# Output stages of a two-layer decoder trunk: three last slabs interleaved by token tile, and four next slabs split during the norm

## The chip, the cores and the metric

The kernel runs on one core of one Trainium2 chip. The metric is the device time of one execution in microseconds (us). The names used are TensorE (PE, with its weight loads PEld), VectorE (DVE), ScalarE (ACT), GpSimd (POOL) and SyncE (SP), which issues the loads of the weight stream.

## The reference

For each of two layers, on x of 512 tokens by 1024 features in float32:

```python
proj = x @ w_in[l]                      # then three mixers: state-space, pooling, sparse attention
merged = sum(gate * branch_d)           # per-channel sigmoid gates
x = layer_norm(ALPHA * x + merged @ w_out[l], g, b)
h_gate, h_up = split(x @ ffn_w_in[l])   # 2816 wide each
x = layer_norm(ALPHA * x + (silu(h_gate) * h_up) @ ffn_w_out[l], g, b)
```

There are four products that end in a layer norm (n = 0 to 3): the two output stages of each layer.

## The kernel before

Every engine has its own program, with an order written out by hand; each runs its instructions strictly in that order, and semaphores tie them together. Nothing is planned at run time.

**The weight stream.** All large weights come as 264 slabs of 128 x 1024 float32 (512 KB), numbered through both layers. SP loads slab c + 2 into `raw[c % 2]` as soon as VectorE has made the low part of slab c (line 396). Products are made of float32r parts: ScalarE copies a slab into `whi` (`split_hi`, line 973), VectorE subtracts (`split_lo`, line 1373) and writes `wlo`. Both have two slots, by the parity of the slab. `split_hi(c)` waits until TensorE is done with slab c - 2 (`slab_done`). A product of a slab takes 24 matmuls: high by high, high by low, low by high.

**The output stage** (`to_tokens`, line 587). The result is wanted by token: four token tiles of 128 tokens, and two feature halves of 512 columns, so eight PSUM banks. Slabs hold weights of two blocks of input rows for one feature half. All slabs of half 0 come first, then those of half 1. A slab visits the four token tiles with 6 matmuls each (`token_products`). Only the last two slabs (called a and b in the code) are interleaved: a and b on tiles 0 and 1, a on tiles 2 and 3, b on tile 2, the turn-back of tokens 0 and 1, b on tile 3.

**The norm** (`ln_part`, lines 1009 and 1478) runs beside that. Half 0 means token tiles 0 and 1, half 1 tiles 2 and 3. VectorE takes the statistics of a tile's second 512 columns (`second_stats`), aggregates, ScalarE takes the root (`deviations`), VectorE inverts (`scalars`); then VectorE normalizes the first 512 columns (`first_columns`) and ScalarE the others (`normalized`; in half 1 of a norm that is not the last, both). `turn_back` (line 575) transposes 16 blocks to feature order in PSUM, ScalarE applies gain and shift (`gained`, line 997), VectorE splits x into `xh` and `xl` (`halves`, line 1461). Each gives four quarters of two feature blocks.

**The next slabs.** The first two slabs after a norm are computed by quarters (`first_pair`, `x_quarter`, line 543): 6 matmuls of 256 columns each, as soon as a quarter of x for one half of the tokens is split. Order: four quarters of slab 0, turn-back of half 1, four of slab 1, then the second half's four of slab 0 and four of slab 1. The splits of these two slabs stand inside `ln_part`; those of the following two stand after it. Then come whole slabs (`x_slab`, line 537).

**POOL in layer 1.** Behind the norm n = 1, POOL issues the loads of `w1` (2 x 2 MB, read by the compression products, line 673) when the last slab of layer 0 is done, then the store of x to memory when the norm is done, then computes the powers of the state-space poles (lines 476 to 506, `lam` and `eph`). VectorE reads them for matrices and for the scan (line 1687), whose result TensorE multiplies at lines 736 and 742.

Of the kernel before, what the change touches and what calls it, by code (L numbers as in the profile page):

```python
# [16 lines left out]
D, S, L, P = 1024, 512, 2, 128  # L17
# [55 lines left out]
def build_program(nc, wstream, w1s, smalls, norms, consts, xin, pos, out):  # L73
# [45 lines left out]
    gates = place("gates", big_at, [P, 16, S])  # L119
    xt = place("xt", xf_at, [P, 4, D])  # L120
# [134 lines left out]
    with ctx:  # L255
# [155 lines left out]
        def _(pool):  # L411
# [44 lines left out]
            for l in range(L):  # L456
# [69 lines left out]
        def _(pe):  # L526
# [16 lines left out]
            def x_quarter(n, half, g, x_before):  # L543
# [4 lines left out]
                for k in (2 * g, 2 * g + 1):  # L548
                    wh, wl = whi[:, n % 2, k * P:k * P + P], wlo[:, n % 2, k * P:k * P + P]
# [14 lines left out]
            def token_products(slot, fh, t, k0, hi, lo, last):  # L564

                dst = ps[:, tile_bank(fh, t), :]
                for q in range(2):
                    a, b = hi[:, k0 + q, P * t:P * t + P], lo[:, k0 + q, P * t:P * t + P]
                    wh, wl = whi[:, slot, S * q:S * q + S], wlo[:, slot, S * q:S * q + S]
# [17 lines left out]
            def to_tokens(n, at, pairs, hi, lo, freed, taken, each, rt):  # L587

                for fh in range(2):
# [3 lines left out]
                    for s in range(pairs - 2 * fh):  # L593
# [4 lines left out]
                        for t in range(4):  # L598
                            m = token_products(c % 2, fh, t, 2 * s, hi, lo, fh == 0 and s == pairs - 1)
# [1548 lines left out]
```

## Time and profile before

| | |
|---|---|
| timed runs | 1765.88 us median of 3 (1765.68 to 1766.67) |
| span of the profiled execution | 1767.2 us (the profile gives no other time of this execution) |
| TensorE matmul busy | 1733.0 us (98%), 10172 instructions |
| VectorE busy | 944.0 us (53%) |
| ScalarE busy | 649.2 us (37%) |
| POOL busy | 125.6 us (7%) |
| mean granted TensorE clock | 0.997 |

Times are from the start of the span. Matmuls are pipelined: one lasts 0.39 us in the trace, while the next starts earlier, so spacing between starts is what counts. The granted clock is a share of 2.4 GHz.

### The profile page before, as it was taken

What the parts mean: (1) busy time and instruction counts of PE and PEld (TensorE: products, weight loads), DVE (VectorE), ACT (ScalarE), POOL (GpSimd) and SP (SyncE); (2) the same over time, 40 slices, a digit from 0 to 9 for tenths busy, and PEclk for the clock granted to TensorE, in tenths of its full rate; (3) what the DMA queues carried; (4) which work ended last, traced back from release to release, by engine and by line L of the source; (5) the groups of instructions that cost most, each with busy time, mean ns of one, the idle gap of its engine ahead of it and who ended that gap; (6) DMA issues with size and microseconds to landing.
All of it is one profiled execution on the core that took longest, in us unless ns stands there. A gap on an engine that the chain in (4) does not pass through costs nothing.

```text
span 1767.2 us, 26801 instructions
## 1 busy us (share of the span) xinstructions
PE 1733.0 (98%) x10172; PEld 1409.5 (80%) x10172; DVE 944.0 (53%) x1514; ACT 649.2 (37%) x1152; POOL 125.6 (7%) x252
## 2 busy tenths in 40 slices
PE   7999999999999999999999999999999999999998
PEld 6778777788888888888888777777888888888886
DVE  5788778444354444422358877775453544444223
ACT  4333666422252222221353346664222522222112
POOL 4700000000000000000037000000000000000000
PEclk9999999999999999999999999999999999999999
DMA  7443111133513222222263431112233222222222
GB/s 259 157 117 88 53 50 49 49 101 102 169 63 105 95 95 95 95 96 95 91 244 110 116 86 50 53 37 72 96 119 119 82 98 95 95 95 95 96 96 83
DMA packets 65918, 174.88 MB, mean 99 GB/s; under 512 B 14256, under 2 KB 26576, under 8 KB 65056
## 3 DMA queue, kind: packets, MB, share of 16 engines
q1 hardware_dynamic: 40192, 140.53, 24.5%
q10 hardware_dynamic: 21888, 13.64, 3.2%
q0 software_dynamic: 3744, 19.41, 3.2%
q8 instruction: 66, 1.08, 0.3%
q14 instruction: 28, 0.23, 0.1%
HBM read 162.27 MB, written 7.08 MB: 96 GB/s over the span
## 4 chain that ended last, share of the span: by engine, by line
PE 86%; DVE 7%; DVEq 3%; ACT 2%; issue 1%; DMA 0%; ACTq 0%
PE ps L532 19%; PE ps L534 18%; PE ps L533 18%; PE ps L572 6%; PE ps L570 6%; PE ps L571 6%; PE ps L857 2%; PE ps L844 2%; PE ps L830 1%; DVE wlo L1376 1%; PE ps L550 1%; PE ps L561 1%; PE ps L552 1%; PE ps L551 1%; PE ps L583 1%
## 5 line engine op out<-in xcount | busy, mean ns | idle before, releaser
L532 PE MATMUL ps<-xh,whi 128*128 128x512 f32 x1312 | 520.0, 396 | 8.4 <-ACT gates L1190 5.1
L534 PE MATMUL ps<-xh,wlo 128*128 128x512 f32 x1312 | 511.3, 390 | 0.0
L533 PE MATMUL ps<-xl,whi 128*128 128x512 f32 x1312 | 510.9, 389 | 0.0
L1376 DVE TENSOR_TENSOR wlo<-raw,whi 128x1024 fp32r<-128x1024 f32 x264 | 324.9, 1231 | 347.4 <-ACT whi L977 338.2
L977 ACT ACTIVATE whi<-raw 128x1024 fp32r<-128x1024 f32 x264 | 278.9, 1057 | 351.0 <-PE ps L572 234.3
L532 PEld LDWEIGHTS ps<-xh,whi 128*128 128x128 f32 x1312 | 246.4, 188 | 61.4 <-issue 7.8
L534 PEld LDWEIGHTS ps<-xh,wlo 128*128 128x128 f32 x1312 | 246.3, 188 | 52.3
L533 PEld LDWEIGHTS ps<-xl,whi 128*128 128x128 f32 x1312 | 246.6, 188 | 48.8 <-issue 0.5
L570 PE MATMUL ps<-whi,hh 128*128 128x512 f32 x352 | 137.5, 391 | 0.0
L572 PE MATMUL ps<-whi,hl 128*128 128x512 f32 x352 | 137.0, 389 | 0.0
L571 PE MATMUL ps<-wlo,hh 128*128 128x512 f32 x352 | 137.0, 389 | 0.0
L1360 ACT ACTIVATE hh<-fb 128x512 f32 (+1 forms) x44 | 27.8, 632 | 201.8 <-DVE fb L1382 201.8
L1382 DVE TENSOR_TENSOR fb<-fa,ps 128x512 f32<-128x512 f32 x44 | 30.2, 687 | 110.9 <-PE ps L534 110.7
L416 POOL TENSOR_TENSOR carry<-carry 1x1 f32<-1x1 f32 x21 | 5.2, 248 | 1176.2 <-PE ps L572 419.5
L1977 DVE SCALAR_TENSOR_TENSOR fa<-ft,ps 128x512 f32<-128x512 f32 x44 | 30.3, 688 | 99.5 <-ACT ft L1357 99.5
L572 PEld LDWEIGHTS ps<-whi,hl 128*128 128x128 f32 x352 | 66.1, 188 | 13.8
L570 PEld LDWEIGHTS ps<-whi,hh 128*128 128x128 f32 x352 | 66.1, 188 | 13.7 <-DVE wlo L1376 0.3
L571 PEld LDWEIGHTS ps<-wlo,hh 128*128 128x128 f32 x352 | 66.1, 188 | 13.6
L1357 ACT ACTIVATE ft<-ps 128x512 f32<-128x512 f32 x44 | 26.3, 598 | 132.7 <-PE ps L534 128.7
L1255 ACT ACTIVATE prob<-ps,tiny 128x128 f32<-128x128 f32 (+3 forms) x128 | 66.3, 525 | 20.4 <-DVE tiny L1802 20.3
L1802 DVE TENSOR_REDUCE tiny<-ps 128x2 f32<-128x256 f32 (+3 forms) x64 | 52.4, 819 | 11.8 <-PE ps L833 11.8
L550 PE MATMUL ps<-xh,whi 128*128 128x256 f32 x128 | 39.5, 309 | 15.7 <-DVE wlo L1376 9.9
(338 smaller groups left out, 2335.5 us busy)
## 6 DMA issues: line engine op xcount, KB each, us to landing
raw<-wstream SPq DMA_DIRECT2D x264, 512.0 KB, 3.3
w<-w1s POOLq DMA_DIRECT2D x4, 2048.0 KB, 11.7
sm<-smalls POOLq DMA_DIRECT2D x2, 1060.0 KB, 6.7
xt<-xin ACTq DMA_DIRECT2D x4, 512.0 KB, 6.3
scratch_u<-pa ACTq DMA_DIRECT2D x8, 256.0 KB
toep<-scratch_k ACTq DMA_DIRECT2D x4, 512.0 KB
toep_b<-scratch_k ACTq DMA_DIRECT2D x4, 512.0 KB
xt<-xin POOLq DMA_DIRECT2D x4, 512.0 KB, 4.0
```

What stands on the lines that cost most here:

```text
L532: pe.matmul(ps[:, bank, :], wh, hi[:, k, :], start=first and i == 0, stop=False)
L533: pe.matmul(ps[:, bank, :], wh, lo[:, k, :], start=False, stop=False)
L534: m = pe.matmul(ps[:, bank, :], wl, hi[:, k, :], start=False, stop=last and i == len(blocks) - 1)
L550: pe.matmul(dst, wh, xh[:, k, cols], start=k == 0, stop=False)
L570: pe.matmul(dst, a, wh, start=False, stop=False)
L571: pe.matmul(dst, a, wl, start=False, stop=False)
L572: m = pe.matmul(dst, b, wh, start=False, stop=last and q == 1)
L844: m = pe.transpose(ps[:, bank, at + P * k:at + P * k + P], prob[:, i % 3, kv, P * k:P * k + P], ident)
L977: act.activation(whi[:, c % 2, :], raw[:, c % 2, :], ACT.Copy).then_inc(hi_ready, 1)
L1255: x = act.activation(prob[:, i % 3, kv, 0:n], ps[:, sbank(i) + kv, 0:n], ACT.Exp, bias=tiny[:, 28 + 8 * (i % 3) + kv:29 + 8 * (i % 3) + kv ...
L1376: dve.tensor_tensor(wlo[:, c % 2, :], raw[:, c % 2, :], whi[:, c % 2, :].bitcast(f32), SUB).then_inc(lo_ready, 1)
L1802: dve.tensor_reduce(tiny[:, 28 + 8 * (i % 3):30 + 8 * (i % 3)], ps[:, sbank(i):sbank(i) + 2, 0:n], AX.X, MAX, negate=True).then_inc(s_max, 1)
```

## The change

The two parts of slab storage get three further slots, `whi_end` and `wlo_end`, in memory that the stage has finished with. The last slab of a stage goes to slot 0, the first two slabs after it to slots 1 and 2; all three are split before the norm's instructions on ScalarE and VectorE. The two slabs after those (b+3, b+4) are split inside the norm, in the ordinary slots. On TensorE the last three slabs are interleaved: tiles 0 and 1 of each, then tile 2 of all, the turn-back of half 0, then tile 3 of all. The pair after it takes the first quarter of its second slab ahead of the turn-back of half 1, and visits both slabs quarter by quarter in the second half. In half 1, VectorE normalizes the first columns, as in half 0. POOL stores x first and loads `w1` after slab 1 of layer 1. The last stage has no next slabs. Layer 0's first pair keeps its order (`first_slabs`). The diff, without the edits that only pass arguments or repeat one shown:

```diff
@@ -117,6 +117,8 @@
+    whi_end = place("whi_end", big_at, [P, 3, 1024], f32r)
+    wlo_end = place("wlo_end", big_at + 3072, [P, 3, 1024], f32r)
@@ -465,13 +467,11 @@
                 if l:
-                    wait(slab_done, l * NSLAB + 2)
-                    load_w1()
-
-                if l:
                     wait(ln_x, l * 16)
                     for t in range(4):
                         pool.dma_start(scr_x[:, t, :], xt[:, t, :]).then_inc(x_stored, 16)
+                    wait(slab_done, l * NSLAB + 4)
+                    load_w1()
@@ -546,7 +546,10 @@
-                    wh, wl = whi[:, n % 2, k * P:k * P + P], wlo[:, n % 2, k * P:k * P + P]
+                    if x_before:
+                        wh, wl = whi_end[:, 1 + n % 2, k * P:k * P + P], wlo_end[:, 1 + n % 2, k * P:k * P + P]
+                    else:
+                        wh, wl = whi[:, n % 2, k * P:k * P + P], wlo[:, n % 2, k * P:k * P + P]
@@ -574,8 +577,7 @@
-                if half == 0 or n == 2 * L - 1:
-                    pe.wait_ge(ln_first, n + half + 1)
+                pe.wait_ge(ln_first, n * 2 + half + 1)
                 pe.wait_ge(ln_second, n * 4 + 2 + 2 * half)
@@ -590,43 +592,57 @@
-                    for s in range(pairs - 2 * fh):
+                    for s in range(pairs - 3 * fh):
                         c = at + fh * pairs + s
                         pe.wait_ge(lo_ready, c + 3)
...
-                a, b = at + 2 * pairs - 2, at + 2 * pairs - 1
-                k = 2 * pairs - 4
-                pe.wait_ge(lo_ready, a + 3)
-                for t in (0, 1):
-                    token_products(a % 2, 1, t, k, hi, lo, False)
-                pe.wait_ge(lo_ready, b + 3)
-                for t in (0, 1):
-                    token_products(b % 2, 1, t, k + 2, hi, lo, True).then_inc(t_psum, 1)
-                for t in (2, 3):
-                    m = token_products(a % 2, 1, t, k, hi, lo, False)
-                m.then_inc(slab_done, 1)
-                token_products(b % 2, 1, 2, k + 2, hi, lo, True).then_inc(t_psum, 1)
+                b = at + 2 * pairs - 1
+                ends = ((whi[:, (b - 2) % 2, :], wlo[:, (b - 2) % 2, :]), (whi[:, (b - 1) % 2, :], wlo[:, (b - 1) % 2, :]), (whi_end[:, 0, :], wlo_end[:, 0, :]))
+                k = 2 * pairs - 6
+                for s in range(3):
+                    pe.wait_ge(lo_ready, b - 2 + s + 3)
+                    for t in (0, 1):
+                        m = token_products(ends[s][0], ends[s][1], 1, t, k + 2 * s, hi, lo, s == 2)
+                        if s == 2:
+                            m.then_inc(t_psum, 1)
+                for s in range(3):
+                    m = token_products(ends[s][0], ends[s][1], 1, 2, k + 2 * s, hi, lo, s == 2)
+                m.then_inc(t_psum, 1)
                 turn_back(n, 0, rt)
-                token_products(b % 2, 1, 3, k + 2, hi, lo, True).then_inc(slab_done, 1)
+                for s in range(3):
+                    token_products(ends[s][0], ends[s][1], 1, 3, k + 2 * s, hi, lo, s == 2).then_inc(slab_done, 1)
+
...
             def first_pair(n, at, rt):
 
-                pe.wait_ge(lo_ready, at + 3)
+                pe.wait_ge(lo_ready, at + 4)
                 for g in range(4):
                     x_quarter(at, 0, g, n * 8)
-                if n:
-                    turn_back(n - 1, 1, rt)
-                pe.wait_ge(lo_ready, at + 4)
+                x_quarter(at + 1, 0, 0, n * 8)
+                turn_back(n - 1, 1, rt)
+                for g in range(1, 4):
+                    x_quarter(at + 1, 0, g, n * 8)
                 for g in range(4):
-                    x_quarter(at + 1, 0, g, n * 8)
-                for c in range(2):
-                    for g in range(4):
+                    for c in range(2):
                         m = x_quarter(at + c, 1, g, n * 8)
-                    m.then_inc(slab_done, 1)
+                        if g == 3:
+                            m.then_inc(slab_done, 1)
@@ -634,7 +650,10 @@
-                first_pair(l * 2, l * NSLAB, xt)
+                if l:
+                    first_pair(l * 2, l * NSLAB, xt)
+                else:
+                    first_slabs()
@@ -976,6 +995,26 @@
+            def split_end_hi(c, slot, free):
+
+                act.wait_ge(raw_loaded[c % 2], (c // 2 + 1) * 16)
+                act.wait_ge(slab_done, free + 3)
+                act.activation(whi_end[:, slot, :], raw[:, c % 2, :], ACT.Copy).then_inc(hi_ready, 1)
...
+            def split_next_hi(c, free):
+
+                act.wait_ge(raw_loaded[c % 2], (c // 2 + 1) * 16)
+                act.wait_ge(slab_done, free + 3)
+                act.activation(whi[:, c % 2, :], raw[:, c % 2, :], ACT.Copy).then_inc(hi_ready, 1)
...
+            def stage_splits(at, pairs, last):
+
+                b = at + 2 * pairs - 1
+                split_end_hi(b, 0, b - 3)
+                if not last:
+                    split_end_hi(b + 1, 1, b - 3)
+                    split_end_hi(b + 2, 2, b - 3)
@@ -989,10 +1028,8 @@
-                    for fh in (0, 1) if half and n < 2 * L - 1 else (1,):
-                        x = act.activation(rt[:, t, S * fh:S * fh + S], ps[:, tile_bank(fh, t), :], ACT.Identity,
-                                           bias=lnnb[:, t:t + 1], scale=lnrs[:, t:t + 1])
-                    x.then_inc(ln_second, 1)
+                    act.activation(rt[:, t, S:], ps[:, tile_bank(1, t), :], ACT.Identity, bias=lnnb[:, t:t + 1], scale=lnrs[:, t:t + 1])\
+                       .then_inc(ln_second, 1)
@@ -1011,16 +1048,16 @@
                 deviations(n, 0)
                 normalized(n, 0, rt)
-                if not last:
-                    split_hi(0, next_slab)
                 for g in range(4):
                     gained(n, 0, g, rt, last)
+                if not last:
+                    split_next_hi(next_slab + 2, next_slab - 2)
                 deviations(n, 1)
-                if not last:
-                    split_hi(0, next_slab + 1)
                 normalized(n, 1, rt)
                 for g in range(4):
                     gained(n, 1, g, rt, last)
+                if not last:
+                    split_next_hi(next_slab + 3, next_slab - 2)
@@ -1063,9 +1100,11 @@
-                a1_split(1)
+                if l == 0:
+                    a1_split(1)
                 a1_out(1)
-                a1_split(2)
+                if l == 0:
+                    a1_split(2)
@@ -1342,15 +1381,16 @@
-                for c in range(1, NO):
+                for c in range(1, NO - 1):
                     split_hi(0, l * NSLAB + OO + c)
                     if c == 1:
                         merged_hi(3)
+                stage_splits(l * NSLAB + OO, KD // 2, False)
                 ln_part(l * 2, l * NSLAB + OF, xt)
...
-                        if not (first and c == 0):
+                        if not first or c == 3:
@@ -1363,8 +1403,9 @@
-                for c in range(1, NG):
+                for c in range(1, NG - 1):
                     split_hi(0, l * NSLAB + OG + c)
+                stage_splits(l * NSLAB + OG, KF // 2, l == L - 1)
@@ -1374,6 +1415,11 @@
+            def split_end_lo(c, slot):
+
+                dve.wait_ge(hi_ready, c + 1)
+                dve.tensor_tensor(wlo_end[:, slot, :], raw[:, c % 2, :], whi_end[:, slot, :].bitcast(f32), SUB).then_inc(lo_ready, 1)
@@ -1490,25 +1536,18 @@
                 first_columns(0)
                 second_stats(n, 2, next_slab + 2)
-                if not last:
-                    split_lo(0, next_slab)
-                halves(n, 0, 0, rt, last)
-                if last:
-                    halves(n, 0, 1, rt, last)
+                for g in range(4):
+                    halves(n, 0, g, rt, last)
                 second_stats(n, 3, next_slab + 2)
                 variances(1)
-                if last:
-                    scalars(n, 1)
-                    first_columns(1)
-                    halves(n, 0, 3, rt, last)
-                else:
-                    halves(n, 0, 1, rt, last)
-                    scalars(n, 1)
-                    for g in (2, 3):
-                        halves(n, 0, g, rt, last)
-                    split_lo(0, next_slab + 1)
+                scalars(n, 1)
+                first_columns(1)
+                if not last:
+                    split_lo(0, next_slab + 2)
                 for g in range(4):
                     halves(n, 1, g, rt, last)
+                if not last:
+                    split_lo(0, next_slab + 3)
@@ -1562,11 +1601,10 @@
-                a1_lo(1)
                 if l == 0:
+                    a1_lo(1)
                     angles()
-                a1_lo(2)
-                if l == 0:
+                    a1_lo(2)
@@ -1956,20 +1994,25 @@
-                def stage(at, pairs, last_low=False):
-                    for c in range(1, 2 * pairs):
+                def stage(at, pairs, last_low=False, last=False):
+                    b = at + 2 * pairs - 1
+                    for c in range(1, 2 * pairs - 1):
                         if c == pairs + 1:
                             first_stats(at + pairs + 2)
                         split_lo(0, at + c)
                         if c == 1 and last_low:
                             low_parts(3)
+                    split_end_lo(b, 0)
+                    if not last:
+                        split_end_lo(b + 1, 1)
+                        split_end_lo(b + 2, 2)
```

## Rows read from the trace of the kernel before

**Rows 1.** The list of waits of TensorE: engine, line, releaser: us in total, times, longest.

```profile
PE ps L550 <- DVE xl L1382: 5.6, 8, 1.3
```

**Rows 2.** ScalarE in order of time (start us, us, what, wait and releaser), splits of b-1, b.

```profile
493.14 1.06 ACT L977 ACTIVATE whi<-raw 128x1024 fp32r<-128x1024 f32 x1 [6.14 <-PE ps L572]
...
864.20 1.06 ACT L977 ACTIVATE whi<-raw 128x1024 fp32r<-128x1024 f32 x1 [4.38 <-PE ps L572]
...
1368.24 1.06 ACT L977 ACTIVATE whi<-raw 128x1024 fp32r<-128x1024 f32 x1 [6.14 <-PE ps L572]
1373.68 1.06 ACT L977 ACTIVATE whi<-raw 128x1024 fp32r<-128x1024 f32 x1 [4.38 <-PE ps L572]
```

**Rows 3.** TensorE in order of time, the first full slab after each of three norms.

```profile
528.41 0.50 PE L532 MATMUL ps<-xh,whi 128*128 128x512 f32 x1
...
899.75 0.50 PE L532 MATMUL ps<-xh,whi 128*128 128x512 f32 x1
...
1402.59 0.50 PE L532 MATMUL ps<-xh,whi 128*128 128x512 f32 x1
```

**Rows 4.** TensorE in order of time, the turn-back of half 1 in the first norm.

```profile
517.86 1.91 PE L583 MATMUL ps<-cn,xt 128*128 128x128 f32 x16
519.52 0.36 PE L550 MATMUL ps<-xh,whi 128*128 128x256 f32 x1
```

**Rows 5.** Windows: stretch, its us, busy us of each engine (instructions), granted clock, DMA share, GB/s.

```profile
514.20:517.60 3.40, 3.40 (x16) 3.10 (x15) 3.14 (x5) 2.76 (x4) 0.00 (x0) 0.50 0.02 5
1760.10:1763.50 3.40, 3.40 (x16) 3.04 (x15) 1.59 (x4) 1.79 (x4) 0.00 (x0) 0.50 0.39 130
1763.50:1764.00 0.50, 0.04 (x1) 0.00 (x0) 0.42 (x1) 0.25 (x1) 0.00 (x0) 1.00 0.87 277
```

**Rows 6.** VectorE in order of time, the first norm.

```profile
494.23 1.23 DVE L1376 TENSOR_TENSOR wlo<-raw,whi 128x1024 fp32r<-128x1024 f32 x1 [4.74 <-ACT whi L977]
...
504.01 0.70 DVE L1443 BATCH_NORM_STATS2 lnst<-ps 128x6 f32<-128x512 f32 x1 [0.39 <-PE ps L572]
...
505.83 1.53 DVE L1483 TENSOR_SCALAR xt<-ps,lnmv,lnrs 128x512 f32<-128x512 f32 x2
```

**Rows 7.** ScalarE in order of time, the gains of half 1 in the first norm.

```profile
518.49 3.75 ACT L1006 ACTIVATE xt<-ps,nrm 128x256 f32<-128x256 f32 x8 [1.53 <-PE ps L583]
```

**Rows 8.** SP's loads of slabs (line 396) from 480 to 532 us.

```profile
DMA to landing us min/median/max: 3.1/3.2/3.3
```

**Rows 9.** POOL in order of time, layer 1, and the powers' last instruction in layer 0.

```profile
882.33 0.18 POOL L416 TENSOR_TENSOR carry<-carry 1x1 f32<-1x1 f32 x1 [419.54 <-PE ps L572]
...
898.49 1.25 POOL L416 TENSOR_TENSOR carry<-carry 1x1 f32<-1x1 f32 x1 [14.94 <-issue]
...
910.75 0.18 POOL L416 TENSOR_TENSOR carry<-carry 1x1 f32<-1x1 f32 x1 [8.90 <-issue]
...
964.96 0.13 POOL L506 MEMSET r8m<- 128x16 f32 x1
...
92.14 0.13 POOL L506 MEMSET r8m<- 128x16 f32 x1
```

**Rows 10.** VectorE in order of time, matrices and scan of layer 1.

```profile
943.93 1.11 DVE L1382 TENSOR_TENSOR tb<-lam,bch 128x512 f32<-128x512 f32 x1
...
965.81 0.68 DVE L1382 TENSOR_TENSOR tb<-lam,bch 128x512 f32<-128x512 f32 x1
...
977.28 1.42 DVE L1382 TENSOR_TENSOR sct<-eph,ps 128x256 f32<-128x256 f32 x4 [0.16 <-issue]
```

**Rows 11.** TensorE in order of time: compression (L673) and Toeplitz (L736) products, both layers.

```profile
65.99 1.36 PE L673 MATMUL ps<-w,zb 128*64 128x256 f32 x10
...
109.01 1.15 PE L736 MATMUL ps<-toep,u 128*64 128x64 f32 x32 [0.66 <-issue]
...
941.92 1.36 PE L673 MATMUL ps<-w,zb 128*64 128x256 f32 x10
...
983.33 1.15 PE L736 MATMUL ps<-toep,u 128*64 128x64 f32 x32 [0.27 <-issue]
```

More of the change, by code:

```diff
@@ L562, in residual, with token_products @@
                                   start=m == 0, stop=False, is_transpose=True)
-            def token_products(slot, fh, t, k0, hi, lo, last):
+            def token_products(high, low, fh, t, k0, hi, lo, last):
                 dst = ps[:, tile_bank(fh, t), :]
@@ L568, in token_products @@
                     a, b = hi[:, k0 + q, P * t:P * t + P], lo[:, k0 + q, P * t:P * t + P]
-                    wh, wl = whi[:, slot, S * q:S * q + S], wlo[:, slot, S * q:S * q + S]
+                    wh, wl = high[:, S * q:S * q + S], low[:, S * q:S * q + S]
                     pe.matmul(dst, a, wh, start=False, stop=False)
@@ L598, in to_tokens @@
                         for t in range(4):
-                            m = token_products(c % 2, fh, t, 2 * s, hi, lo, fh == 0 and s == pairs - 1)
+                            m = token_products(whi[:, c % 2, :], wlo[:, c % 2, :], fh, t, 2 * s, hi, lo, fh == 0 and s == pairs - 1)
                         m.then_inc(slab_done, 1)
-                a, b = at + 2 * pairs - 2, at + 2 * pairs - 1
-                k = 2 * pairs - 4
-                pe.wait_ge(lo_ready, a + 3)
-                for t in (0, 1):
-                    token_products(a % 2, 1, t, k, hi, lo, False)
@@ new lines, in to_tokens, with first_slabs @@
+                for s in range(3):
+                    m = token_products(ends[s][0], ends[s][1], 1, 2, k + 2 * s, hi, lo, s == 2)
+                m.then_inc(t_psum, 1)
+                turn_back(n, 0, rt)
+                for s in range(3):
+                    token_products(ends[s][0], ends[s][1], 1, 3, k + 2 * s, hi, lo, s == 2).then_inc(slab_done, 1)
+            def first_slabs():
+                pe.wait_ge(lo_ready, 3)
+                for g in range(4):
+                    x_quarter(0, 0, g, 0)
+                pe.wait_ge(lo_ready, 4)
+                for g in range(4):
+                    x_quarter(1, 0, g, 0)
+                for c in range(2):
+                    for g in range(4):
+                        m = x_quarter(c, 1, g, 0)
+                    m.then_inc(slab_done, 1)
@@ L624, in first_pair @@
                 for g in range(4):
-                    x_quarter(at + 1, 0, g, n * 8)
-                for c in range(2):
-                    for g in range(4):
+                    for c in range(2):
                         m = x_quarter(at + c, 1, g, n * 8)
-                    m.then_inc(slab_done, 1)
+                        if g == 3:
+                            m.then_inc(slab_done, 1)
             ident = cnv("ident")
@@ L1492, in ln_part @@
                 second_stats(n, 2, next_slab + 2)
[L1493 to L1497 removed]
+                for g in range(4):
+                    halves(n, 0, g, rt, last)
                 second_stats(n, 3, next_slab + 2)
                 variances(1)
[L1500 to L1509 removed]
+                scalars(n, 1)
+                first_columns(1)
+                if not last:
+                    split_lo(0, next_slab + 2)
                 for g in range(4):
                     halves(n, 1, g, rt, last)
+                if not last:
+                    split_lo(0, next_slab + 3)
             dve.memset(tiny[:, 0:1], 0.0).then_inc(lo_ready, 2)
@@ L1971, in ff_pairs @@
                     for c in range(4):
-                        if not (first and c == 0):
+                        if not first or c == 3:
                             split_lo(h, c + 1)
@@ L1991, in _ @@
                     ff_pairs(hl_ + OF // 2 + 2 + i * 2, i + 1, False)
-                stage(l * NSLAB + OG, KF // 2)
+                stage(l * NSLAB + OG, KF // 2, last=l == L - 1)
                 ln_part(l * 2 + 1, (l + 1) * NSLAB, xt)
```

## Prediction

> **What bounds the kernel now.** I read the page first: TensorE is busy 98% of the span, so only what stands between its matmuls, or what slows them, can be taken away. Next the list of waits: in the norms TensorE waits for the split x, 5.6 us in 8 waits [rows 1]. Then the order of time at each norm. Call b the last slab of an output stage, b-1 and b-2 the two before, b+1 to b+4 the next four. ScalarE's split of b-1 is released when slab b-3 is done; I call that moment T: 493.14, 864.20 and 1368.24 for the first three norms [rows 2]. The first full slab after the norm starts at 528.41, 899.75 and 1402.59 [rows 3]. So the stretch takes 35.27, 35.55 and 34.35 us.
>
> Its pure work: three slabs of 24 matmuls at 5.44 us each (1368.24 to 1373.68, one slab [rows 2]) = 16.32; 16 quarters of 6 matmuls, 256 columns each, at 8.89/72 = 0.1235 (519.52 to 528.41 [rows 3, 4], hand-over included) = 11.85; two blocks of 16 transposes, 1.66 each (517.86 to 519.52 [rows 4]) = 3.32. Sum 31.5 us. What is above it is 3.8, 4.05 and 2.85 us of idle time and slow clock. In the first norm the granted clock is 0.50 from 514.20 to 517.60, that is 1.2 of 2.4 GHz, right after its waits for x [rows 5].
>
> **The change, part by part.**
>
> *The weave (TensorE).* No matmul is added or removed; 72 + 96 + 32 instructions stay in each stretch. New order from T: token tiles 0 and 1 of all three slabs (36 matmuls, 8.16 us), tile 2 of all (18, 4.08), the turn-back of half 0, tile 3 of all (18, 4.08), then five quarters, turn-back of half 1, three quarters, eight quarters. Before, only 6 matmuls (1.36 us) stood between turn-back and the first quarter, which needs the turned, gained and split x; now 18 do. Work in three slots means that b-1 must be split by T+2.72. Its low part began at 494.23 and takes 1.23 [rows 6]: T+2.3. It fits, with 0.4 us to spare.
>
> *Splits of b, b+1, b+2 ahead of the norm (ScalarE, VectorE, SP).* Both engines are in order, and the three splits now stand before the first statistics. The high part of b follows that of b-1 at once, its low part runs T+2.2 to T+3.45. Each low part releases SP's load of the slab two later; issue to landing is 3.2 us [rows 8]. b+1: issue T+2.5, landing T+5.7, high part to T+6.8, low part to T+8.1. b+2: issue T+3.65; the two transfers overlap, I take landing T+7.1, high part to T+8.2, low part to T+9.45. Only then does VectorE take the first statistics. Their data are there at T+6.8, so they are 2.7 us late. From the start of the second statistics (504.01) to the end of the first columns (505.83 + 1.53) it takes 3.35 us [rows 6]; the first statistics add 0.97 (0.70, the aggregate and its gaps). The turn-back can start at T+9.45+0.97+3.35 = T+13.8. TensorE is there at T+12.24. **New wait: 1.5 us in each of three norms**, on the path. Queued behind it on TensorE is everything. Bounds: below, 0.5 us (both loads land as if alone and the splits close up); above, 3 us (the second load lands 1.5 us later).
>
> *After the turn-back.* Gained x comes at 3.75/4 = 0.94 us a quarter [rows 7], starting 0.63 after the turn-back's start (517.86 to 518.49 [rows 4, 7]): T+15.4 to T+18.2; VectorE needs 1.1 each, all ready at T+19.8. TensorE ends tile 3 at T+19.6 and its fourth quarter needs the last at T+21.7: no wait. Tile 3's end (T+19.6) releases the fourth statistics; VectorE is free at T+19.8, plus 3.35: turn-back 1 at T+23.2. TensorE arrives after five quarters at T+23.2. I take 0 here, bounds 0 and 0.5. Second half: x ready from T+26, TensorE comes at T+27: no wait. ScalarE's wait for slab b-1 (T+18.2) falls on the end of its gains: nothing. The splits of b+3 and b+4 lie in ScalarE's and VectorE's gaps (done by T+24.4 and T+30.5; first needed at T+33). The first columns moved from ScalarE to VectorE in half 1: 1.53 against two activations, both in the 3.35 chain.
>
> *New stretch:* 31.5 + 1.5 = 33.0. Gains: 2.3, 2.55, 1.35 = **6.2 us**. The last norm has no next slabs, so no late statistics, and tile 3 ends when the same 72 matmuls are done: its tail stays. Layer 0's start is unchanged.
>
> *POOL's order in layer 1.* Before, the w1 loads went first (882.33, next POOL instruction 898.49: 16.16 us), then the x store (to 910.75: 12.26), then the powers, done at 964.96 + 0.13: 54.3 us [rows 9]. Now the store waits for the last gain, at T+27.7 with T at 864.20 - 2.3 = 861.9, so 889.6; store to 900.8 (POOL is already idle, so 11.1 without its wake), w1 to 917.0, powers to **971.3**. It was 965.1. TensorE's clockwork is 2.3 + 2.55 = 4.85 earlier by then, so POOL is 11 us later against it. VectorE's scan uses the powers at 977.28 [rows 10], now wanted at 972.4: 1.1 us spare. But VectorE is the tight engine here, and POOL slows it: the same 128x512 multiply takes 1.11 us at 943.93 beside POOL and 0.68 at 965.81 after it [rows 10]. POOL's largest operations move onto the second pair of matrices and the slab splits just before the scan, while the first pair gets free of them; the early gain is eaten by a wait for ScalarE, the late loss (some 2.4 us on six operations, 0.7 won back) is not. I take **1.7 us lost**. Bounds: 0 (the contention only moves), and 5.6 by layer 0: there POOL ends 26.2 after the compression matmuls begin and TensorE reaches the Toeplitz products after 43.0; in layer 1, 23.1 and 41.4 [rows 9, 11]; so 1.6 us lost for 3.1 of POOL, and 11 us at that rate cost 5.7. I lean to the low end because the late operations are few.
>
> The Trainium skill (SBUF — State Buffer, Who interferes with whom) states that the port pair of VectorE and GpSimd is an exclusive lock held for a whole instruction; the stretched 1.11 us agrees. By that rule alone total blocking is conserved when POOL's work moves, and the term would be near 0.
>
> *Sum:* 6.2 - 1.7 = 4.5 us. The profiled span, 1767.2, is 1.3 above the median of the timed runs; a difference of stretches carries over: 1765.9 - 4.5 = **1761.4**.
>
> **Rivals.**
> A. *Weave as forecast, with little lost in layer 1, or loads that land early.* 6.2 + 1.5 at most: 1758 to 1760. For it: the spare 1.1 us, conserved contention. Chance 0.25.
> B. *The clock falls in the new wait.* 1.5 us idle, then 1.66 of transposes, then 18 matmuls at 1.2 GHz. A half-clock stretch did 16 matmuls in 3.40 us [rows 5] that take 1.98 at full clock: 1.4 to 1.7 lost each. Three times: 1761.4 + 4.7 = 1766, no change. Against: a norm has 1.9 us of waits for x before (5.6 in three [rows 1]), in pieces, more than the new 1.5; and from 1760.10 to 1763.50 TensorE did nothing but 16 transposes at 0.50, after which the clock stood at 1.00 [rows 5]. Chance 0.15. The Trainium skill (TensorE: Matmul & The Clock Gate, Part 4: PE-mode transpose) says that transposes don't count as busy for the clock gate; by that rule this rival would be the likeliest. The trace speaks against it: the clock rose on transposes alone.
> C. *The wait at the turn-back is 3 us, or the layer-1 loss is 4 to 5.* 1763.5 to 1765.5. Chance 0.15.
> D. *Slower: POOL becomes the bound of layer 1.* Store, w1 and powers stand in one row, 81.7 us, behind the norm. If a quarter slower than before, by loads that share the DMA engines and by VectorE's port, they end 20 us later, at 991, and the scan, with everything on TensorE behind it, slips 19: 1765.9 - 6.2 + 19 = 1779. It decides from the point where POOL ends 7.3 us later than I work out, at 978.6. Against: both waits and the powers have rows of their own. Chance 0.05.
> My forecast (1760.5 to 1763) has 0.40.
>
> **How the numbers follow.** 0.2%, 3.5 us, is about what a measurement tells from no change. Faster means under 1762.4: A, most of the forecast's 0.40 and little of the rest: 0.69. Same: B, C and what is left: 0.25. Slower: 0.06, mostly D. Range 1757.5 to 1765.5: it leaves out D, half of B and the very best of A.
>
> **What would show it.** In the chain at each of three norms, VectorE's low part of b+2 ends 9.4 us after T and the first statistics follow without idle; the transposes wait about 1.5 us; no quarter waits for x; no half clock before the last norm; stretches of 33.0 us. In layer 1 POOL's last memset near 971 and the Toeplitz products 41.4 + 1.7 us after the compression matmuls begin. I am wrong if the transposes don't wait, if a stretch exceeds 34, or if those products come over 46 us after.

## The result: 1774.9 us, slower by half a per cent

The changed kernel took 1774.86 us (median of 4 runs, 1774.54 to 1776.7), the kernel before 1766.22 beside it: ratio 1.0051 [1.0039, 1.0064]. The forecast was 1761.4, range 1757.5 to 1765.5. The profiled span is 1774.9 (before 1767.2); TensorE is busy 1735.1 us (1733.0 before), the mean granted clock 0.994 (0.997). Every other profiled execution was timed too, and its time is its span + 1.8 us; by that (an estimate) the profiled execution of before took 1769.0, 2.8 above its median, and that of the changed kernel, at 1776.7, 1.8 above its own. So the profiles differ by 7.7 us and the timed medians by 8.6.

TensorE's waits after. The row of x [rows 1] is gone; the 11.1 us hold 3.6 of the last norm's tail, so 7.5 are new waits ahead of three turn-backs:

```profile
PE ps L585 <- ACT xt L1031: 11.1, 4, 3.6
PE ps L553 <- DVE wlo L1417: 9.4, 1, 9.4
PE ps L532 <- issue: 6.5, 2, 4.7
```

**First norm.** ScalarE in order of time; the first row is T [rows 2]:

```profile
494.79 1.06 ACT L996 ACTIVATE whi<-raw 128x1024 fp32r<-128x1024 f32 x1 [6.14 <-PE ps L575]
495.75 1.04 ACT L1002 ACTIVATE whi_end<-raw 128x1024 fp32r<-128x1024 f32 x1
500.50 1.06 ACT L1002 ACTIVATE whi_end<-raw 128x1024 fp32r<-128x1024 f32 x1 [3.70 <-DMA raw<-wstream]
502.78 1.06 ACT L1002 ACTIVATE whi_end<-raw 128x1024 fp32r<-128x1024 f32 x1 [1.22 <-DMA raw<-wstream]
```

VectorE: the low part of b+2, the first statistics right behind it, the first columns [rows 6]:

```profile
503.87 1.23 DVE L1422 TENSOR_TENSOR wlo_end<-raw,whi_end 128x1024 fp32r<-128x1024 f32 x1 [1.05 <-ACT whi_end L1002]
505.01 0.69 DVE L1489 BATCH_NORM_STATS2 lnst<-ps 128x6 f32<-128x512 f32 x1
...
507.67 1.52 DVE L1529 TENSOR_SCALAR xt<-ps,lnmv,lnrs 128x512 f32<-128x512 f32 x2
```

TensorE: turn-back of half 0, of half 1, next full slab [rows 3, 4]:

```profile
509.38 2.91 PE L585 MATMUL ps<-cn,xt 128*128 128x128 f32 x16 [2.41 <-ACT xt L1031]
...
520.60 1.94 PE L585 MATMUL ps<-cn,xt 128*128 128x128 f32 x16
...
530.29 0.40 PE L532 MATMUL ps<-xh,whi 128*128 128x512 f32 x1
```

The wait is where it was forecast, at T+14.6 in place of T+13.8, and 2.41 us in place of 1.5. The second turn-back waits for nothing, as forecast, and so do all quarters. But the first turn-back takes 2.91 us for what takes 1.94 at the second: the clock has fallen. Windows of the changed kernel (as in [rows 5]), one in each norm and the third in layer 1's mixers (columns: stretch, its us, busy us of PE, PEld, DVE, ACT, POOL with their instructions, granted clock, DMA share, GB/s):

```profile
510.10:513.50 3.40, 3.40 (x16) 3.11 (x14) 2.25 (x5) 3.40 (x8) 0.00 (x0) 0.51 0.00 0
882.20:885.60 3.40, 3.40 (x13) 2.82 (x12) 2.80 (x6) 3.08 (x7) 0.00 (x0) 0.50 0.01 2
984.70:988.10 3.40, 3.40 (x9) 2.62 (x9) 3.15 (x8) 0.00 (x0) 0.00 (x0) 0.51 0.44 154
1390.90:1394.30 3.40, 3.40 (x15) 3.11 (x14) 2.30 (x5) 3.40 (x8) 0.00 (x0) 0.51 0.02 5
```

So the first stretch took 530.29 - 494.79 = 35.5 us, forecast 33.0, before 35.27.

**Layer 0.** The clock also fell at 104.0, behind this wait, where before has no fall and no wait above 1 us:

```profile
103.14 0.47 PE L532 MATMUL ps<-xh,whi 128*128 128x512 f32 x1 [1.84 <-issue]
```

**Layer 1.** POOL in order of time: the instruction just ahead of the x store, of w1, of the powers, and the powers' end [rows 9]:

```profile
896.58 0.66 POOL L418 TENSOR_TENSOR carry<-carry 1x1 f32<-1x1 f32 x1 [432.20 <-ACT xt L1043]
...
905.77 0.18 POOL L418 TENSOR_TENSOR carry<-carry 1x1 f32<-1x1 f32 x1 [6.43 <-issue]
...
923.16 0.18 POOL L418 TENSOR_TENSOR carry<-carry 1x1 f32<-1x1 f32 x1 [15.82 <-issue]
...
982.90 0.13 POOL L506 MEMSET r8m<- 128x16 f32 x1
```

The powers end at 982.90, forecast 971.3, before 965.09. VectorE, last matrix of the second pair and the slab split behind it [rows 10]:

```profile
975.41 1.70 DVE L1428 TENSOR_TENSOR wmat_b<-ta,tb 128x576 f32<-128x576 f32 x1
...
981.81 2.05 DVE L1417 TENSOR_TENSOR wlo<-raw,whi 128x1024 fp32r<-128x1024 f32 x1
```

TensorE waits for that split. Compression, slab, Toeplitz [rows 11]: 992.09 - 945.66 = 46.4 us; before 41.4, forecast 43.1.

```profile
945.66 0.72 PE L692 MATMUL ps<-w,zb 128*64 128x256 f32 x4
...
983.96 0.47 PE L532 MATMUL ps<-xh,whi 128*128 128x512 f32 x1 [4.69 <-issue]
...
992.09 1.15 PE L755 MATMUL ps<-toep,u 128*64 128x64 f32 x32
```

### The profile page after: what moved, and what is told of

It is laid out like the page before. It is cut to its first block, busy times and chain, and to the rows that moved or that the text cites. A ratio compares the mean times of both kernels' runs of the same rounds, so it can differ in the third digit from the quotient of the medians.

```text
span 1774.9 us, 26801 instructions
## 1 busy us (share of the span) xinstructions
PE 1735.1 (98%) x10172; PEld 1412.0 (80%) x10172; DVE 946.6 (53%) x1520; ACT 646.5 (36%) x1146; POOL 131.8 (7%) x252
## 4 chain that ended last, share of the span: by engine, by line
PE 86%; DVE 6%; ACT 2%; DVEq 2%; DMA 2%; issue 1%; SPq 0%; ACTq 0%
PE ps L532 19%; PE ps L534 18%; PE ps L533 18%; PE ps L573 5%; PE ps L575 5%; PE ps L574 5%; PE ps L876 2%; PE ps L863 2%; DMA raw<-wstream 1%; PE ps L849 1%; PE ps L585 1%; PE ps L553 1%; PE ps L554 1%; PE ps L555 1%; DVE wlo L1417 1%
## 5 line engine op out<-in xcount | busy, mean ns | idle before, releaser
L1417 DVE TENSOR_TENSOR wlo<-raw,whi 128x1024 fp32r<-128x1024 f32 x254 | 313.5, 1234 | 337.0 <-ACT whi L996 331.3
L996 ACT ACTIVATE whi<-raw 128x1024 fp32r<-128x1024 f32 x248 | 262.1, 1057 | 337.3 <-PE ps L575 216.7
L573 PE MATMUL ps<-whi,hh 128*128 128x512 f32 x336 | 131.9, 393 | 0.0
L575 PE MATMUL ps<-whi,hl 128*128 128x512 f32 x336 | 131.2, 391 | 0.0
L574 PE MATMUL ps<-wlo,hh 128*128 128x512 f32 x336 | 131.2, 390 | 0.0
L876 PEld LDWEIGHTS ps<-probt,vtok 128*64 128x64 f32 x640 | 33.6, 136 | 23.0 <-issue 23.0
## 6 DMA issues: line engine op xcount, KB each, us to landing
w<-w1s POOLq DMA_DIRECT2D x4, 2048.0 KB, 14.2
```

The source lines that it names most:

```text
L573: pe.matmul(dst, a, wh, start=False, stop=False)
L574: pe.matmul(dst, a, wl, start=False, stop=False)
L575: m = pe.matmul(dst, b, wh, start=False, stop=last and q == 1)
L876: pe.matmul(ps[64 * kv:64 * kv + 64, 7, P * t:P * t + P], vtok[:, br, k, 64 * kv:64 * kv + 64], probt[:, i % 2, kv, P * k:P * k + P], star ...
L996: act.activation(whi[:, c % 2, :], raw[:, c % 2, :], ACT.Copy).then_inc(hi_ready, 1)
L1417: dve.tensor_tensor(wlo[:, c % 2, :], raw[:, c % 2, :], whi[:, c % 2, :].bitcast(f32), SUB).then_inc(lo_ready, 1)
```

## The experiments

In the table a norm is the time from VectorE's low part of slab b-1 to the low part six slabs on (ten in norm 2); "mixers" are the fourteen slabs behind norm 1. All from one profiled execution each, us. Falls: norms of three in which the clock fell to 0.50. The median is of timed runs.

| kernel | norm 0 | norm 1 | norm 2 | falls | mixers | median |
|---|---|---|---|---|---|---|
| before | 41.54 | 41.81 | 62.36 | 2 | 101.12 | 1766.2 |
| after | 41.65 | 42.27 | 63.39 | 3 | 105.98 | 1774.9 |
| e7, after again | 41.86 | 42.94 | 61.92 | 2 | 105.78 | 1774.7 |
| e6, fill | 40.05 | 42.10 | 61.99 | 0 | 108.07 | 1772.1 |
| e11, no powers | 39.84 | 42.75 | 63.24 | 2 | 101.80 | 1768.9 (1 run) |
| e2, w1 early | 41.76 | 42.52 | 61.89 | 2 | 100.52 | 1767.8 |
| e5, w1 by ScalarE | 41.58 | 42.58 | 63.09 | 3 | 98.17 | 1767.6 |
| e1, low part later | 38.53 | 39.12 | 59.79 | 0 | 106.16 | 1764.8 |
| e3, e1 and e2 | 38.39 | 39.31 | 59.95 | 0 | 100.48 | 1759.6 |
| e8, e3 and splits inside | 38.68 | 38.62 | 60.05 | 0 | 99.10 | 1758.9 |
| e9, e1 and e5 | 38.56 | 38.74 | 59.96 | 0 | 98.16 | 1758.8 |
| e10, e8's splits and e5 | 38.65 | 38.59 | 60.06 | 0 | 98.17 | 1757.4 |
| e4, before, w1 late | 41.70 | 41.89 | 62.36 | 2 | 102.94 | 1771.9 |
| e12, before, w1 by ScalarE | 42.26 | 42.35 | 62.37 | 1 | 96.42 | 1765.6 |

The experiments were timed in three groups (e1 to e4, e5 to e8, e9 to e12), each beside the kernel before (1765.9, 1766.9 and 1766.6 us); a ratio is to before's runs of the same group.

**e1.** VectorE's low part of b+2 goes behind tile 2's statistics:

```diff
-                        split_end_lo(b + 2, 2)          # ahead of the first statistics
...
                 second_stats(n, 2, next_slab + 2)
+                if not last:
+                    split_end_lo(next_slab + 1, 2)
```

> The changed kernel, with one line of VectorE moved: the low part of slab b+2 is made behind the third tile's statistics and not ahead of the first's. Its trace had, in each of three norms, 2.4 us of waiting ahead of the turn-back and then 3.4 us at 0.50 of the clock; the first statistics began at T+10.3, when the low part of b+2 was done. Theory N (the order on VectorE makes the wait, the wait makes the clock fall): the statistics begin near T+8.1, the turn-back near T+12.5, no wait above 0.5 us, no half clock in the first three norms; stretches of 31.7 to 32.2 instead of 35.5, 3.4 us gained three times: 1774.9 - 10 = about 1764.5 to 1765.5. Rival W (the weave as such costs it: the wait moves to the quarters or to the second turn-back): stretches stay at 34.5 or more, 1772 to 1775. Rival K (the clock falls on the transposes, with or without a wait before them): the wait goes and the half clock stays, 1768 to 1769.

Ratio to before 0.9995 [0.9986, 1.0004]; 10 us less than the changed kernel. TensorE, both turn-backs of its first norm:

```profile
504.85 1.94 PE L585 MATMUL ps<-cn,xt 128*128 128x128 f32 x16 [0.47 <-ACT xt L1031]
514.86 0.41 PE L585 MATMUL ps<-cn,xt 128*128 128x128 f32 x2 [0.37 <-ACT xt L1031]
```

The wait is 0.47 in place of 2.41 (in norm 1, 1.12 stay of 2.70) and no norm has a fall. The three norms lose 3.12 + 3.15 + 3.60 = 9.9 us against the changed kernel: one 1.2-us instruction in the wrong place cost that much. 5.1 of it is the waits at the turn-backs (7.5 us, now 2.4), the other 4.8 three half clocks of 1.6. The mixers stay at 106: the second loss is another one.

**e2.** POOL's old order (w1 first); the first two slabs of layer 1 get memory of their own, so that w1 needn't wait (that part of the edit isn't shown):

```diff
+                    wait(slab_done, l * NSLAB + 2)
+                    load_w1()
                     wait(ln_x, l * 16)
...
-                    wait(slab_done, l * NSLAB + 4)
-                    load_w1()
```

> The changed kernel, with POOL's order of before (w1 first, behind the last slab of layer 0, then the x store); the two next slabs of layer 1 lie in other memory, so that w1 can be loaded that early. Theory P (the later w1 load costs layer 1 twice: POOL's powers end 18 us later and slow VectorE, and a slab's load lies behind w1's): POOL ends near 965 to 968 instead of 982.9, no wait of ScalarE for a slab's load above 1 us, the distance from the compression to the Toeplitz products is 41.5 again instead of 46.4; 1774.9 - 5 to 6.5 = 1768.5 to 1770. Rival L (layer 1 is late because the first pair ends both slabs at once and ScalarE's and VectorE's order in it changed): 1774 to 1775, POOL early and the distance the same.

1767.79 us, ratio 1.0007 [0.9998, 1.0016]. The mixers go from 105.98 to 100.52, the norms stay: POOL's order is the second loss, and the two are separate.

**e3**, both edits together:

> Both edits in one kernel. If theories N and P hold and don't share a cause, the gains add: 10 and 5.5 off 1774.9, about 1759.5 (1757.5 to 1761.5), which would be 6 to 7 us below the kernel before. If either is wrong it comes out at 1764 to 1770.

1759.6, ratio 0.9959 [0.9946, 0.9973]: faster than both kernels. The change does save TensorE's time once its two costs are gone: the norms take 8.1 us less than before's. No run tells the weave's part in this from that of the moved splits or of the first columns on VectorE.

**e4**, the kernel before with POOL's new order alone:

> The kernel before, with POOL's new order alone: x store first, then w1 behind the second slab of layer 1. Nothing else changes. Theory P: POOL ends near 977 to 982 instead of 965, the Toeplitz products of layer 1 come 3 to 5 us later: 1766.2 + 3 to 6 = 1769 to 1772. Rival L: 1766 to 1767.5.

1771.86, ratio 1.0035 [1.0021, 1.0049]. POOL's order alone makes the old kernel slower; its mixers show +1.8 with this wait of TensorE and a half clock behind it:

```profile
PE ps L530 <- issue: 2.7, 1, 2.7
```

The timed difference is 6.0 us, that of the spans 2.0 (1769.2 - 1767.2). The profiled executions make up the rest: that of before (1769.0 by the estimate above) is 3.1 above the median of before's runs beside e4, 1765.9, and e4's, at 1770.97, is 0.9 below its own. So the rows of before come from one of its longer executions; where the 3 us lie in it, no second profile tells.

**e5.** The changed kernel, w1 issued by ScalarE in layer 1:

```diff
-                    wait(slab_done, l * NSLAB + 4)      # POOL
-                    load_w1()
...
                 if l:
+                    for j in range(2):                  # ScalarE
+                        act.dma_start(w1[:, j, :], w1s[...]).then_inc(w1_next[j], 16)
                     first_powers()
```

> The changed kernel, except that the w1 loads of layer 1 (4 MB) are issued by ScalarE's queue right after the last gains, so POOL only stores x and then makes the powers. Theory P (POOL comes late because it stands blocked 17 us on the issue of w1): the powers end near 966 instead of 982.90, VectorE's scan is in time, the wait of 4.69 us ahead of it and the half clock behind it (some 1.7) go, while the slab load that lands late beside w1 (ScalarE's wait of 4.5, TensorE's of 1.33) stays: 1774.9 - 4 to 5 = 1770 to 1771, layer 1's mixers 106.0 -> 101.5. Rival C (the lateness comes from the collision of the w1 transfer with the slab loads, wherever it is issued): VectorE stays late by its splits, the mixers stay at 105 to 106 us, 1774.

1767.55, 7.3 us less than the changed kernel, more than I expected (4 to 5): the mixers went from 105.98 to 98.17. Of this, 4.7 and 1.3 are the two waits of TensorE and 1.6 the half clock. Against before it is a tie: ratio 1.0000 [0.9991, 1.0009]. The wait for the slab behind w1 went too, which I had thought would stay. ScalarE's queue issued both loads in 1.49 us, and ScalarE went on at 901.71, where POOL stood 17.4 (905.77 to 923.16):

```profile
900.17 1.49 ACTq L1109 DMA_DIRECT2D w<-w1s  x2
```

But the issue is not what holds POOL. The two DMA instructions take it 1.10 us in the changed kernel (906.24); it starts again 0.2 us after the second load has landed (922.94), and so in every one of the 24 pairs of w1 loads that POOL issues in the 14 profiles. Before that restart the program has `pool.drain()`, in layer 1 as the first line of its `wait` helper. In layer 0 an instruction without a drain ahead of it ran right behind the issue, and the next, behind a drain, 0.2 us after the landing at 54.74:

```profile
35.20 0.28 POOL L492 COPY eph<-php 128x32 f32<-128x32 f32 x1
54.97 0.21 POOL L444 TENSOR_TENSOR st<-eph 128x16 f32<-128x16 f32 x1 [19.48 <-issue]
```

So the rows point to the drain: POOL's pause is the transfer's length. No run leaves the drain out, which might be the smaller repair; e5 shows only that taking w1 out of POOL's row is enough.

POOL's last memset comes at 955.93, and VectorE's last matrix no longer shares the time with it:

```profile
971.30 0.76 DVE L1429 TENSOR_TENSOR wmat_b<-ta,tb 128x576 f32<-128x576 f32 x1
```

**e11** leaves out the doubling steps of the powers in layer 1 (that part is set to zero):

> The changed kernel with the doubling steps of the powers left out in layer 1 (that part of the powers is set to zero; POOL still waits, stores x and loads w1). Theory P (POOL's powers beside VectorE, and their end at 982.9, are what the late w1 costs through): VectorE's six matrix operations go from 1.4-1.7 us to 0.7-0.8, the wait of 4.7 and the half clock behind it go, layer 1's mixers 106 -> under 99. Rival C (the collision of the w1 transfer with slab loads): the mixers stay above 103.

The wait of 4.7 us and its half clock are gone, the matrices take 0.76; but the mixers are at 101.8, between the two theories. What is left is the slab behind w1: TensorE waits, and the clock falls:

```profile
931.82 0.67 PE L535 MATMUL ps<-xh,whi 128*128 128x512 f32 x1 [1.81 <-DVE wlo L1420]
```

```profile
932.10:935.50 3.40, 3.40 (x9) 2.63 (x9) 3.40 (x5) 0.67 (x2) 3.12 (x4) 0.51 0.70 217
```

That half clock is e11's own: the changed kernel's profiles have the slab's wait (1.33 and 1.24) and no fall behind it. So 105.98 is not to be split at 101.80. From the waits it is 98.17 + 4.69 + 1.6 (the half clock at 984.6) + 1.33 = 105.8: the late powers cost 6.3, the slab load behind w1 1.3. And e11 is 98.17 + 1.81 + 1.6 = 101.6 of its 101.80. Issued by ScalarE at 900.17, w1 costs neither.

**e6.** Tile 3 of slab b-2 ahead of the turn-back:

```diff
                 m.then_inc(t_psum, 1)
+                token_products(ends[0][0], ends[0][1], 1, 3, k, hi, lo, False).then_inc(slab_done, 1)
                 turn_back(n, 0, rt)
-                for s in range(3):
+                for s in range(1, 3):
```

> The changed kernel, with the 6 matmuls (1.36 us) of token tile 3 of slab b-2 put ahead of the turn-back of half 0: no wait is taken away from VectorE's chain, but the single wait of 2.4 us becomes 1.05 us before the turn-back, and the rest comes back as some 1.3 us elsewhere (ahead of the turn-back of half 1, whose statistics start earlier or later by as much). Theory L (one long wait followed by transposes alone is what makes the clock fall): no half clock in the three norms, a stretch of about 33.8 us in place of 35.5, so 1774.9 - 3 x 1.7 = 1770. Rival K (the clock falls after any wait ahead of the transposes, or the fall comes from elsewhere): half clock stays, 1774 to 1775.

1772.08, ratio 1.0027 [1.0018, 1.0037], between the two forecasts. No norm has a fall. Norm 0 is 1.6 us shorter with as much wait in all (1.00 + 1.38), which is the price of a half clock. Norms 0 and 2 (waits of 1.00 and 1.17) are as theory L has it. Norm 1 is not: its wait of 2.73 is longer than the one I blamed, and the transposes run at full clock all the same. One norm of that kind, where 3 of 15 stay without a fall in the changed order anyway, neither shows theory L nor refutes it:

```profile
507.48 1.94 PE L585 MATMUL ps<-cn,xt 128*128 128x128 f32 x16 [1.00 <-ACT xt L1032]
517.14 1.94 PE L585 MATMUL ps<-cn,xt 128*128 128x128 f32 x16 [1.38 <-ACT xt L1032]
...
878.78 1.94 PE L585 MATMUL ps<-cn,xt 128*128 128x128 f32 x16 [2.73 <-ACT xt L1032]
```

In its mixers the clock fell twice (near 932 and 983), once more than in the changed kernel: they are 2.1 us longer, of the 3.2 that the norms gained.

**e7**, the changed kernel again:

> The changed kernel as it is, once more, for its scatter: the time 1775, and one more look at layer 0, where the program is that of before. Theory S (layer 0's +1.65 us is scatter of POOL's w1 load, 20.9 us in the profile of the changed kernel and 15.1 in that of before): the start of the first stage's slab 20 lies anywhere between 148 and 151, with POOL's powers moving with it. Rival: it is fixed, 150.6 again.

1774.68. Layer 0 is back at 149.18 for slab 20 (150.65 in the first profile, 149.00 before; over all kernels 148.0 to 150.7): those 1.65 us were scatter, and the trace shows which. In the first profile layer 0's second w1 load landed at 54.74 (50.0 to 50.5 in the other 13), the last instruction of POOL's powers came at 98.25 (92.14 before), VectorE's operations beside them stretched, and TensorE had the wait of 1.84 and the half clock shown above: the same chain as in layer 1. In place of it a fall near 1184, where nothing was changed, cost 1.6. And its norm 2 has the same wait as the first profile without a fall:

```profile
1391.06 1.94 PE L585 MATMUL ps<-cn,xt 128*128 128x128 f32 x16 [2.47 <-ACT xt L1031]
```

**e8.** e3, with the high part of b+2 behind the first normalized columns, the low part of b+1 behind the first columns:

> The kernel that joins both repairs (low part of slab b+2 behind the statistics of tile 2; w1 early into other memory), and beside them: ScalarE's high part of b+2 behind the first normalized half-columns, VectorE's low part of b+1 behind the first columns and that of b+2 behind tile 2's statistics. Theory V (the last waits of 0.47 and 0.37 us ahead of the turn-backs hang on ScalarE's table load behind the high part of b+2): both go, 1.2 us in three norms or somewhat more, 1759.6 -> 1758.3. Rival: the split that is moved inside makes the quarters wait for x or the next slab for its low part, and the time stays at 1759.6 or is some us more.

1758.86. The rival's outcome holds, by another mechanism: the three norms take 137.35 us, in e3 137.65, because the wait has moved from the first turn-back to the second (1.18, 0.83 and 0.81 us). What e3's profile lost to e8's was a fall near 1171 outside all edits (1.5 us) and 1.4 in the mixers.

**e9** and **e10**: e1 with e5, and e8's splits with e5.

> The changed kernel with two repairs that use no further memory: VectorE's low part of slab b+2 behind tile 2's statistics, and the w1 loads of layer 1 issued by ScalarE. If the two losses (the norms' order on VectorE, POOL's blocked time) are separate, their repairs add: 1774.9 - 10 (the first alone) - 7.3 (the second alone) = 1757.5. Rival: the earlier TensorE needs the powers and the slab loads earlier too, the mixers of layer 1 take 101 us as in the kernel that joins the first repair with an early w1 (100.5) in place of 98.2, and it ends at 1760.

> As the kernel with both repairs and the splits of b+1 and b+2 moved inside the norm, but w1 issued by ScalarE, no other memory for the slabs. Its forerunner took 1758.9 with layer 1's mixers at 99.1 us; with 98.2 it comes to 1758. Rival: as for the other kernel with w1 on ScalarE, no gain from it or a small loss, 1759 to 1761.

1758.79 (0.9951 [0.9937, 0.9965]) and 1757.35 (0.9946 [0.9932, 0.996]). The repairs add, without further memory, and beat both kernels. e10 has the lowest median, but the intervals of e3, e8, e9 and e10 overlap. Its norms (137.30) and mixers (98.17) equal e9's (137.26, 98.16); e9's profile has another fall, near 1169. In e10 the wait stands at the second turn-back, as in e8:

```profile
505.07 1.91 PE L584 MATMUL ps<-cn,xt 128*128 128x128 f32 x16
515.85 1.94 PE L584 MATMUL ps<-cn,xt 128*128 128x128 f32 x16 [1.18 <-ACT xt L1029]
```

**e12**, the kernel before with w1 by ScalarE:

> The kernel before, with the w1 loads of layer 1 issued by ScalarE's queue after its second output. Theory: there POOL stands blocked 16.2 us by w1 too, ahead of the x store, and its powers end at 965; freed of that they end some 12 us earlier and VectorE gets rid of POOL sooner: the mixers of layer 1 go from 101.1 to about 98.2 as in the changed kernel with the same repair, the time 1766.9 - 2.9 = 1764. Rival: the w1 transfer falls later beside the slab loads and nothing is gained, 1766 to 1767.

No gain is shown: the timed runs say 1765.6, 1.0 below before, ratio 0.9995 [0.9986, 1.0004]. In the profile the mixers are 4.7 us shorter and the two first norms 1.3 longer, 4.0 in the spans, but 2.4 of that is before's long profiled execution (1769.0 against a median of 1766.6) and 0.5 e12's own.

## Why the prediction was wrong

**The weave, forecast -6.2 us; the three norms took +1.6.** Two steps failed, and they account for it: -6.2 + 3.0 + 4.8 = +1.6.

*New wait: 1.5 us in each of three norms.* The mechanism and its place were right. The size was 2.5 (7.5 in three), because the second of two overlapping loads landed at T+8.0, not T+7.1; the chain behind it took what I gave it. That is 3 us, and my upper bound of 3 us a norm held it. e1 shows that two thirds of the wait were not needed: I worked out that the statistics were 2.7 us late and left it at its price.

*Rival B, the clock falls in the new wait, 0.15.* It is what happened, in 3 norms of 3 here, and in 12 of 15 over the five kernels with the changed order. A fall costs 1.6. Less its wait, norm 0 takes 39.84 - 2.15 = 37.7 us in e11, whose norm 0 has the same program and no fall, and 41.65 - 2.41 = 39.2 in the changed kernel with one; norm 2 takes 61.92 - 2.47 = 59.5 in e7 without and 63.39 - 2.38 = 61.0 with one. So 4.8 us; the rival's own price, 1.4 to 1.7, was right and its chance was not. I argued from before's 1.9 us of waits a norm "in pieces", which brought 2 falls in 3 (5 in 9 with e4 and e12); with the pieces gone I counted before's falls as saved and gave the new wait none. In the five kernels with the low part later no norm of 15 has a fall; their longest wait is 1.29.

The other reason against rival B was the row in which the clock rose after transposes alone. It doesn't repeat. All 14 kernels end with the same 16 transposes behind the same wait of 3.56 us. The clock is back at 1.00 after them in four (before, e6, e7, e8); in nine it stays at 0.50 to the end, as in e10 (transposes from 1748.79 to 1752.4), and e12's falls only later:

```profile
1751.30:1756.00 4.70, 1.14 (x6) 0.74 (x4) 1.46 (x4) 1.02 (x2) 0.00 (x0) 0.50 0.67 223
```

The Trainium skill (TensorE: Matmul & The Clock Gate, Part 4: PE-mode transpose) says that transposes don't count as busy for the clock in the way that matmuls do. The falls that begin inside these transposes agree with it, and so do the nine endings at 0.50; the two norms above with waits of 2.47 and 2.73 and no fall show that it doesn't decide alone. Putting it aside on the one row [rows 5] was the mistake.

**POOL's order in layer 1, forecast 1.7 lost; the mixers took 4.9.** The upper bound of 5.7 lay near that by luck: its rate is 1.6 us for 3.1 of POOL, and against the compression matmuls POOL ended 14.2 later than before (983.03 - 945.66 = 37.4, before 23.2), so the rate gives 7.3, with no term for the load. POOL started 7.0 late because norm 0 had gained nothing, layer 0 had lost 1.65 and norm 1 had its longer wait and half clock; its store took 2.0 less than I gave it, its w1 17.4 and its powers 59.9 (16.2 and 54.3 before). It ended at 982.90, past the 978.6 from which rival D decides. But that point moves with TensorE, whose compression matmuls came at 945.66 and not at 941.92 - 4.85 = 937.1: 8.6 later, so D decides from 987.2. D's mechanism, a scan that waits for the powers, didn't come: VectorE has no idle time there, and reads them at 984.78. The failed term is my 2.4 us on six operations: from 972.38 to 981.81 the six of the second pair take 9.43 us, 4.9 more than six of 0.76, and the split behind them 0.8 more than 1.23. I had taken the stretch from one row, 1.11 against 0.68 [rows 10]; here it is 1.70 against 0.76. The Trainium skill (SBUF — State Buffer, Who interferes with whom) states that the port pair of VectorE and GpSimd is an exclusive lock. The rows agree that the blocking moves with POOL's work: in e5 the same stretch falls on the first pair (a 128x512 multiply of 1.54 us) and the second is free of it. What I drew from it, a term near 0 and a lean to the low end, was wrong, because VectorE had time to spare under the first pair (3.51 us idle before 961.42) and none under the second. And one effect had no term: w1, issued later, held a slab's load back (ScalarE waits 4.55, TensorE 1.33). The mixers after are 98.17 + 4.69 + 1.6 + 1.33; before's 101.12 holds 2.4 us of waits of its own, which is why the net loss is 4.9 and not 7.8.

**The rest.** The last norm's tail was forecast at no change and took 0.6 less; layer 0's +1.65 is the late w1 landing and half clock of that execution. +1.6 (norms) + 4.9 (mixers) + 1.65 + 0.25 (between) - 0.6 = 7.8; the spans differ by 7.7.

What stays open: what makes the clock fall in one execution and not in the next after the same wait, where before's profiled execution lost its 2.8 us, and whether taking the drain out of POOL's row would do what e5 does.

## What to carry to other kernels

Work out the order of a busy engine's queue, not only its sum: a split that TensorE needs 12 us later (516.88), put ahead of the statistics that everybody waits for, cost 9.9 us. A new wait ahead of TensorE is to be priced with its half clock (1.6 us here), and one row in which the clock held or rose is not enough to leave it out. A DMA issued from an engine that also computes can cost that engine the whole transfer: look at when its next instruction starts, what stands ahead of it in the program, and whether another queue issues the load without that, before moving it in time.

## What the runs showed of the hardware

The same two loads of 2 MB kept POOL, which then drains, for 15 to 21 us, until 0.2 us after they had landed, and ScalarE's queue for 1.5. The clock's falls are partly chance. Near 96 us, in layer 0, where the program is the same in all kernels, TensorE waits some 2 us; 7 of 14 profiles have a fall behind it, as e10 (first row), and 7 have none, as e5 (second), after an equal wait (1.95 to 2.16 in 13 of them; the changed kernel's first profile waits 1.63, and falls 8 us later behind its second wait):

```profile
95.74 0.80 PE L531 MATMUL ps<-xh,whi 128*128 128x512 f32 x1 [1.97 <-DVE wlo L1419]
```

```profile
95.69 0.50 PE L531 MATMUL ps<-xh,whi 128*128 128x512 f32 x1 [1.98 <-DVE wlo L1418]
```

Three (e3, e7, e9) have one between 1169 and 1184, where the others have none; it costs 1.6 us. The falls near 96 cost nothing that can be told: slab 20 starts at 148.5 to 149.3 with one and at 148.0 to 149.2 without. VectorE is busy there almost without a gap (in e7 from 84 to 110 us) and sets the pace, so TensorE's half clock is hidden. A difference under 2 us between two single profiles of this kernel therefore says nothing until its falls are counted, and even that did not cover the 2.8 us of before's.
